# Grouped attention: a gate tile's evacuation, its weight split and its gating are asked for one part later than its products

## The reference

```python
def gqa_mixer(h, hc, w_in, w_out, qk_g, cos, sin, with_ctx_out):
    def project(t):
        p = t @ w_in
        q, k, v, z = jnp.split(p, [...], axis=-1)
        q = rms_norm(q.reshape(B, L, GQ_HEADS, GQ_HEAD_DIM), qk_g[0])
        ...
    q = apply_rope(q, cos, sin)
    k = apply_rope(k, cos, sin)
    def attend(qq, kk, vv, gate):
        o = sweep_attention(qq, kk, vv)     # softmax(q k^T / sqrt(128)) v
        o = o.reshape(o.shape[0], o.shape[1], BRANCH_WIDTH)
        return (o * jax.nn.silu(gate)) @ w_out
```

## Time and profile before

| | |
|---|---|
| three executions | 1331.42 us median (1330.55 to 1338.41) |
| profiled execution | 1327.89 us, span of its core 1326.1 us |
| granted clock of PE, mean of the span | 0.971 of 2.4 GHz |
| PE busy | 1214.9 us (92%) |
| PEld busy | 1094.5 us (83%) |
| DVE busy | 807.4 us (61%) |
| ACT busy | 583.3 us (44%) |
| POOL busy | 78.8 us (6%) |
| exponentials of the grouped attention | 1219.0 to 1277.3 us of the span |

### The profile page before, as it was taken

How to read it: one execution, slowest core, us unless ns; L and a number is a source line. 1 busy time by engine, 2 the same in 40 slices (tenths; PEclk the granted TensorE clock), 3 DMA queues, 4 the chain that set the end, 5 groups by cost and what they waited for, 6 DMA issues and landing times. The chain is left out here.

```text
span 1326.1 us, 22870 instructions
## 1 busy us (share of the span) xinstructions
PE 1214.9 (92%) x8638; PEld 1094.5 (83%) x8638; DVE 807.4 (61%) x1607; ACT 583.3 (44%) x1066; POOL 78.8 (6%) x87
## 2 busy tenths in 40 slices
PE   4999999988987898999999988999999989998985
PEld 4998899988987897988898987788677779887775
DVE  4865645658947755556565543555666666675764
ACT  4754444453221243533343433554455536554543
POOL 0410000002221000000000000000000000001000
PEclk9999999999988999999999998999999989889998
DMA  5554444443312362377885761111112124312110
GB/s 218 193 181 146 139 148 150 141 131 106 119 64 96 129 209 64 129 255 285 293 288 201 266 238 48 64 65 64 64 49 64 48 75 149 111 65 80 64 49 32
DMA packets 48397, 175.04 MB, mean 132 GB/s; under 512 B 5376, under 2 KB 6016, under 8 KB 47776
## 3 DMA queue, kind: packets, MB, share of 16 engines
q1 hardware_dynamic: 47664, 169.77, 37.8%
q0 software_dynamic: 624, 3.80, 0.8%
HBM read 172.50 MB, written 1.05 MB: 131 GB/s over the span
## 5 line engine op out<-in xcount | busy, mean ns | idle before, releaser
L1643 DVE TENSOR_TENSOR w_lo<-w_raw,w_hi 128x1024 fp32r<-128x1024 f32 (+1 forms) x272 | 330.9, 1223 | 224.9 <-ACT w_hi L1446 186.1
L1446 ACT CAST w_hi<-w_raw 128x1024 fp32r<-128x1024 f32 (+1 forms) x272 | 275.2, 1036 | 92.6 <-PE lin L1156 52.0
L1154 PE MATMUL lin<-XH,w_hi 128*128 128x256 f32 x448 | 129.8, 290 | 2.1 <-DVE w_lo L1643 2.1
L1155 PE MATMUL lin<-XL,w_hi 128*128 128x256 f32 x448 | 127.7, 285 | 0.0
L1156 PE MATMUL lin<-XH,w_lo 128*128 128x256 f32 x448 | 127.7, 285 | 0.0
L1154 PE MATMUL lin<-NH,w_hi 128*128 128x256 f32 x416 | 120.5, 290 | 1.3 <-DVE NL L1777 1.3
L1155 PE MATMUL lin<-NL,w_hi 128*128 128x256 f32 x416 | 117.6, 283 | 0.0
L1156 PE MATMUL lin<-NH,w_lo 128*128 128x256 f32 x416 | 117.6, 283 | 0.0
L1576 ACT ACTIVATE probs<-score,stat 128x512 f32<-128x512 f32 (+1 forms) x88 | 53.0, 607 | 116.6 <-DVE stat L1894 87.0
L1382 POOL TENSOR_TENSOR ms<-ms,mhalf 128x4 f32<-128x4 f32 (+1 forms) x26 | 28.3, 1090 | 1064.3 <-DVE ms L1759 1064.3
L1154 PEld LDWEIGHTS lin<-NH,w_hi 128*128 128x128 f32 x416 | 79.6, 191 | 14.3 <-issue 12.6
(11 more groups left out here) (370 smaller groups left out, 3169.5 us busy)
## 6 DMA issues: line engine op xcount, KB each, us to landing
w_raw<-in_ada SPq DMA_DIRECT2D x48, 512.0 KB, 5.4
w_raw<-in_w_out SPq DMA_DIRECT2D x32, 512.0 KB, 3.3
w_raw<-in_gate SPq DMA_DIRECT2D x22, 512.0 KB, 6.2
w_raw<-in_up SPq DMA_DIRECT2D x22, 512.0 KB, 3.6
w_raw<-in_ffn_out SPq DMA_DIRECT2D x16, 512.0 KB, 3.7
w_raw<-in_q SPq DMA_DIRECT2D x16, 512.0 KB, 3.6
w_raw<-in_z SPq DMA_DIRECT2D x16, 512.0 KB, 3.3
w_raw<-in_k SPq DMA_DIRECT2D x10, 512.0 KB, 3.3
```

The costliest lines, as they stand in the source:

```text
L1154: nc.tensor.matmul(bank[:, 0:W], wh, moving(H, kk), start=first, stop=False)
L1155: nc.tensor.matmul(bank[:, 0:W], wh, moving(L, kk), start=False, stop=False)
L1446: scal.copy(w_hi[:, i % HL, 0:n], raw[:, tile["i"] % RAW, 0:n]).then_inc(w_hi_ready, 1)
L1643: vec.tensor_sub(w_lo[:, i % HL, 0:n], raw[:, tile["i"] % RAW, 0:n], w_hi[:, i % HL, 0:n].bitcast(F32)).then_inc(w_lo_ready, 1)
```

## The change

In turn 2t (part 0) the gate tile's first half of matmuls is made as before. In turn 2t+1 (part 1) only PE has a step: "second", the second half. The "lin" step, which PE now skips for such a tile, stands in turn 2t+2: there ACT casts and evacuates and DVE splits. The gating moves along: that of tile t-2 stands in part 0 of tile t, and behind the "lin" step instead of ahead of it. For the last tile (t = 7) all is in part 1 as before.

```diff
         def fill_gq():
             t, part = divmod(fills_3[0], 2)
             fills_3[0] += 1
-            if part == 1 and t >= 1:
-                gate_3(t - 1)
             if part == 0:
+                if t >= 1:
+                    steps.append(held.pop())
+                if t >= 2:
+                    gate_3(t - 2)
                 lin_step("z_3", t, DT, True, W3x, T, ("act", ZB))
                 held.append(steps.pop())
                 steps.append(("begin", held[0][1]))
+            elif t < GQ_HEADS - 1:
+                steps.append(("second", held[0][1]))
             else:
+                gate_3(t - 1)
                 steps.append(held.pop())
...
-            begun = []
+            begun, ended = [], []
+
+            def second(s):
+
+                ended.append(s["g"])
+                products(s, range(DT // 2, DT))
 
             def linear(s):
                 if "members" in s:
                     if s is s["members"][0]:
                         side_by_side(s["members"])
-                else:
+                elif s["g"] not in ended:
                     products(s, range(DT // 2, DT) if s["g"] in begun else None)
```

More of the change, by code:

```diff
@@ L1359, in hvalues @@
                         last.then_inc(hg_pv, 1)
-            do = {"setup": setup, "lin": linear, "begin": begin, "sq": sq, "sqmm": sq, "bc": bc, "score_mm": score, "transp": transp,
+            do = {"setup": setup, "lin": linear, "begin": begin, "second": second, "sq": sq, "sqmm": sq, "bc": bc, "score_mm": score, "transp": transp,
                   "values": values, "hform": hform, "hvalues": hvalues, "adamm": adamm, "adaturn": adaturn}
```

## The result

Twenty executions of the changed kernel have a median of 1340.25 us (1336.03 to 1348.59), twenty of the kernel before, on the same chip, 1331.04 us (1327.25 to 1339.21). The ratio is 1.0075 (95% interval 1.0060 to 1.0090): slower by about 9 us, less than 1%. Among all executions told of here one, of the kernel before with the load ahead of the exponential, took 1539.29 us; it counts in the median given for that kernel (1325.89 us, 1325.59 without it) and not in its ratio. The profiled execution took 1336.39 us with a span of 1334.6, against 1327.89 and 1326.1 before: +8.5 us.

The account below looks back on a forecast made before the run. The ACT–DVE loop was taken to bound the grouped attention: six pairs +6.24, first pair +0.35, end −0.41, together +6.2 us on the 1331.42 median, 1337.6. Range 1331 to 1342 us.

Parts of the forecast that it names:

- the +2 to +9 that had 80 in 100: Whole kernel: the forecast, with the absorbed clock fall and both bounds in it, 1333.4 to 1340.4 us around the median.
- What bounds the stage: Grouped attention: the loop between ACT's exponential and DVE sets the 8.09 us pair; PE needs 7.29, 0.8 to spare.
- The half that the load leaves: Exponential 6 to 7: nothing left between maximum and reciprocal, 2.53 us instead of 5.56, a gain of 3.03.
- The half that it joins: Exponential 7 to 8: from 2.53 to 6.60 us, by split waiting for ACT's cast, gating 1.59 and QB copy 0.35.
- the lower bound: Wait ahead of the split only the gating's 1.21 us: 0.35 us a pair, +2.0 us in all.
- How many, and the end: Six pairs with gating +6.24 us, first pair +0.35 (7.54), last transposed probabilities' copy earlier, −0.41: together +6.2.
- PE's new wait: Pairs of the stage: PE stops waiting ahead of the values, waits 1.84 us a pair for DVE's probabilities ahead of transposes.
- The output projection then starts as before behind the last split; it and all that follows move along unchanged: Behind the stage: the projection and all after it only shift, with no further cost.
- the prediction's own signs of being wrong: Changed profile: pair of 7.3 or 8.1 us, split 1.2 us after exponential, stage clock 0.50, or difference outside 1219–1291 us.
- PE is the bound: Rival, stage: value products stop waiting, stage runs at PE's 7.29 us a pair, 5.6 us less, 1325.8; 7 in 100.
- No effect: Rival, stage: the wait for the cast grows no more than other waits shrink, 1331.4 give or take 2; 10 in 100.
- The clock in each pair, nothing absorbed: Rival, stage pairs: PE's clock falls in each, 6 × 2.0 = 12 us on top, 1349.6; 3 in 100.

Follow-up runs that it names:

- the load ahead of the exponential: ACT does tanh, cast and evacuation before the turn's exponential, against the kernel before, DVE's order unchanged: 1325.89 us, ratio 0.9964.
- The edit on ACT alone: ACT holds each turn's exponential back until the step "transp", made on the kernel before (1325.89 us) and on the changed kernel (1326.39 us).
- the order with the gating ahead: Changed kernel with the gating put back ahead of the split, both still one part later: 1334.64 us, ratio 1.0029 to before.
- the kernel with the gating apart: Changed kernel with cast, evacuation and split left in part 0, gating of tile t-1 put back in part 1: 1339.29 us, ratio 1.0060 to before.
- all three comparisons: The changed kernel measured three times against the kernel before: ratios 1.0075, 1.0052 and 1.0073.

## Why the prediction was right, and where it was short

It said slower by 6.2 us and within 1%, 1337.6 us; measured were 1338.25, 1340.13 and 1340.25, inside the range of 1331 to 1342, with all three above the likeliest value. Single executions go beyond it, up to 1348.59. Of the differences from before, +7.2, +8.8 and +9.2 us, the last lies just outside the +2 to +9 that had 80 in 100.

**What bounds the stage: right.** The edit on ACT alone took 6.3 us out of the stage of before and 12.3 out of that of the changed kernel, in which PE, the busiest engine, had not a matmul less. PE's own pair is 7.19 us and not 7.29: the values' step to the next start, 1.83 us in the earlier trace rows, is 1.73 where PE never waits (1241.39 to 1243.12 in the first of the two).

**The half that the load leaves: right.** 2.53 us, as the last turn without a load.

**The half that it joins: right.** Forecast 6.60 us, measured 6.57. The wait ahead of the split was read from a single row and is 1.89 us in the steady pair; the lower bound, that it might be no more than the tanh's 1.21, is what the order with the gating ahead gave. The uncovered QB copy is 0.33 where 0.35 was said. A pair: 9.13 forecast, 9.10 measured.

**How many, and the end: right.** First pair 7.54 forecast, 7.52 measured (1224.67 to 1232.19). From the last transposes to the values 1.33 us (1285.90 to 1287.23), and the last split came 6.56 us after where it stood before, of which 0.58 is the later start of the stage. S is +5.98 where the sum said 6.2; six pairs at 1.01 to 1.02 instead of 1.04 are most of that.

**PE's new wait: right in kind.** 1.70 us ahead of the transposes in each pair, 1.84 forecast; the values no longer wait until the last.

**"The output projection then starts as before behind the last split; it and all that follows move along unchanged": this is the step that failed.** The prediction looked at the clock in the pairs alone, +0.2 each if absorbed, and at nothing in the sum; for the end it has no term. But in the pairs it did not fall: the stretch from 1224 to 1282 us is at 1.00 in all five profiles of the changed kernel. It fell at the end of the stage, where the wait for the probabilities is 2.56 us and where no dense products stand behind it: transposes, 0.68 us of wait, values, 1.88 us of wait. There PE is on the path that sets the end, so nothing absorbs it: 1.5 us at the start of the projection, or 2.25 us in the last turn. Two of the prediction's own signs of being wrong are met by this: a difference outside 1219 to 1291 us (in three profiles) and a clock of 0.50 in the stage (in two). They tell against this step and not against the sum of the stage. The profile had shown the place: the last turn's probabilities stand behind the same load as those of a pair, and PE has no next score to make meanwhile, so a wait longer than 1.84 us was to be had from the same sum; and one of 2.27 us had brought the clock to 0.50. The Trainium skill (TensorE: Matmul & The Clock Gate, HAM oscillation) describes a loop whose pauses bring the half clock back in every turn. The pauses of 1.70 us in the pairs of the changed kernel did not, in any of its five profiles. Those of the skill's loop are longer, some 3 to 5 us, so the prediction read too much into it when it said that by that rule each of the six pairs would pay.

How much of the fall behind the stage is the change's own is less sure than that it is the clock's. A fall 12 to 13 us into the projection, at about the same price, comes in kernels with short waits too, and the two profiled executions of before, at 1327.89 and 1327.07 us, lie 3 and 4 us below its medians: those in the middle may well have a fall that no profile shows. The 2.25 us in the last turn stand only in its profiles and lie in its stage, so they are taken as its own; two profiles of before are few to set against them.

**The rivals.** *PE is the bound* was false for the change, yet its time of 1325.8 us and its condition, that the cast be done before the exponential, are what the two ACT edits made true: 1325.89 and 1326.39 us. That the time agrees so well is luck in part: it was made of 5.6 us in the stage, and the stage gave 6.3. *No effect* is out: the intervals of all three comparisons lie above 1, and S is +5.98. *The clock in each pair, nothing absorbed* is out by the clock of 1.00, and the falls in the kernel with the gating apart, absorbed whole, show why it would not have cost 2 us a pair.

**Size, and what stays open.** S and tail together are 115.0, 115.0 and 114.9 us in three profiles of the changed kernel, 116.7 and 116.7 in the two where the clock falls in the last turn, and 107.1 and 107.6 in the two of before: +7.3 to +9.7 us. The medians say +7.2, +8.8 and +9.2, of the same size. The start of the stage lies between 1217.75 and 1224.15 us over all profiles of all kernels: falls of the clock ahead of it, where no kernel was changed, come in some executions and not in others (of the two profiles of before, one has the clock at 0.50 from 1144 to 1151 us), and this scatter is as large as the effect. Shown is the stage's share, 6.0 us, by the profiles and by all executions at an equal clock; and that the other 1 to 3 us go with a lower clock. Open is how much of the lower clock is the change's own: beside before it was 0.9682 against 0.9686 in one comparison and 0.9657 against 0.9691 in the other. Open too is what decides between the two ends, and where the executions of the changed kernel beyond 1345 us lose their time: none of them was profiled.

## What to carry to other kernels

Where two engines hand a small result back and forth, read the time between two hand-overs and list, in the order of each engine, what stands in it; work whose other half runs on the partner engine belongs ahead of the hand-over on that partner, and moving three ACT instructions there was worth more than any order of the two halves behind it. Where a change gives PE a wait that other work absorbs, look for the turn that has no such work, at the end of the loop, and price the clock there and in what follows.

## What the runs showed of the hardware that was not expected

- A wait of PE of 1.70 us in each 9.1 us, behind dense products, left the granted clock at 1.00 through five pairs in each of five profiles, as did the one of 2.00 us at the first transposes. Of four waits of 2.00 and 2.01 us in the pairs of a like loop, two brought it to 0.50 for some 3 us, after which it came back by itself, and two did not; one of 2.07 us elsewhere had left the next product at 0.36 us. The length of the wait alone does not decide.
- With the same instructions and the same wait of 2.56 us at the end, the clock fell ahead of the last transposes in two profiles and only in the projection, 4.7 to 4.8 us after the last values began, in three. A single profile doesn't tell what the end of a stage costs.
- In five profiles of four kernels the clock fell 12 to 13 us into the output projection for some 3 us, 1 to 2 us behind a spell of small sums with a wait of 1.09 or 1.10 us; in the others the same spell brought no fall.
- A fall costs what lies on the path: nothing in the half of the loop that waits for DVE (4.41 and 4.42 us with it, 4.42 without), 1.5 us in the projection, 2.25 us where DVE waits for the values.
